# A transformer block on eight cores: x and modulation by quarters, attention with a row maximum and DMA transposes between the projection groups

## The chip, the cores and the metric

The kernel runs on the 8 cores of one Trainium2 chip. The cores share no work and no data: each takes 1024 of the 8192 tokens with a halo of 128 on either side (core r has sample r // 4, tokens from 1024 (r mod 4)). The metric is the device time of the slowest core in microseconds, the median over runs.

## The reference, cut to what matters

```python
# layer_norm, modulate, adaln as usual; adaln gives shift/scale/gate for mixer and MLP
h_ctx = modulate(ctx, mod_c[:, 0], mod_c[:, 1])
k_ctx, v_ctx = context_kv(h_ctx, w_in[l])
h = modulate(x, mod[:, 0], mod[:, 1])
mix = latent_mixer(h, k_ctx, v_ctx, rope, *mixer_params)
x = layer_norm(ALPHA * x + mod[:, 2] * mix, ln1_g[l], ln1_b[l])
ff = squared_relu_mlp(modulate(x, mod[:, 3], mod[:, 4]), w_ff1[l], w_ff2[l])
x = layer_norm(ALPHA * x + mod[:, 5] * ff, ln2_g[l], ln2_b[l])

def latent_mixer(...):
    q, k, v, u, g = split_projection(h @ w_in)      # 1024, 256, 256, 1024, 1024 columns
    q = axial_rope(q, rope); k = axial_rope(k, rope)
    attn = windowed_attention(q, k, v, k_ctx, v_ctx, sink)
    gm = chunk_spatial_gate(u, g, gln_g, gln_b, w_s, b_s)
    return jnp.concatenate([attn, gm], axis=-1) @ w_out
# windowed_attention: 8 query heads on 2 key heads; a block of 128 queries sees 384 keys
# (|i-j| <= 128 kept) and 256 context keys; one softmax over those and a sink logit.
# chunk_spatial_gate: gelu(u) * (w_s @ layer_norm(gelu(g)) + b_s), 128 positions, 8 heads
```

D_MODEL is 2048, the MLP is 8192 wide, and there is one layer.

## The kernel before

Every engine's work is written out in one order by the host program; buffers record who wrote and read them last, and each operation waits on semaphores for those (on all engines but TensorE also for earlier operations of the same engine). So the order of the source is the order of every engine and of every DMA queue. Weights are f32 in HBM and come as bf16 blocks of 2048 KB, [128, 16, 512], all on the POOL queue through `wload` (L357), into one of four slots W0 to W3 (of three, W0 to W2, from the tenth load on): the one whose last use in the plan is the oldest and that is not in use. A matmul group is 16 matmuls of 128x512 into one PSUM bank (`mm_group`, L320 on; all groups have line L324), and `bank` hands out the eight banks in turn.

- **Modulation.** `ada_chunk` (L427) multiplies one of 24 weight chunks with the two conditioning vectors; VectorE copies the sums (L443) and `ada_stage2` (L404, matmuls L410) turns them into columns. Chunks 4c to 4c+3 make vector c. Chunks 0 to 7 (shift, scale) come first. For a quarter q of the columns chunks q and 4+q are made, then ScalarE modulates four blocks of ctx (HCT) and four of x (HT; `issue_xt`, L451, loads xT on SP's queue into three buffers).
- **K, V, Q.** With chunk 2 of w_in the context's K and V, then ten token blocks of K and V; `rope` (L475) on VectorE, TensorE transposes back to head-major. Then chunks 0 and 1 for Q, 8 blocks each, modulation chunks 8 to 13 between.
- **Attention.** 16 iterations of (token block, key head), four heads at once. `at_s1` (L551) multiplies keys by queries, so that keys lie on the partitions; ScalarE takes exp with no maximum subtracted; VectorE multiplies masks in (L574). `at_s2` (L578), two iterations later, multiplies by V and by a matrix of ones for the denominators; VectorE takes a reciprocal of 128x512 (L594) and multiplies (L596). Modulation chunks 14 to 19 lie between.
- **gMLP.** u: 16 groups and Gelu into GUT. g: per token block two groups, Gelu, statistics, square root on ScalarE, normalized on VectorE (L644, L646), four plus four mixing matmuls (L657), added and multiplied on VectorE (L660, L662). The first four groups of the output projection come at the end of it.
- **Output projection.** `wout_group` (L673) for 4 column blocks x 8 token blocks, evacuated by gate, residual and statistics. The gate as a row on all partitions is made by `gate_bcast` (L716): 16 diagonals on VectorE (L722), 16 f32 matmuls with ones (L725), four copies (L727). x_tm is read by four DMAs, one for each block of 512 columns.
- **MLP.** Four passes; the first holds modulation chunks 22 and 23, both in the slot that the next weight needs, and a second `gate_bcast` before its second half. From the second half of pass 0 on nothing is touched by the change.

## Time and profile before

| | |
|---|---|
| time, median of 3 runs | 1681.81 us (1679.34 to 1687.38) |
| profiled execution: its own time, span | 1682.52 us, 1680.9 us |
| spans of the 8 cores | 1648.1 to 1680.9 us |
| PE busy | 1395.9 us (83%), 6772 matmuls |
| DVE busy | 661.5 us (39%), 1018 instructions |
| ACT busy | 266.8 us (16%), 444 |
| moved by the DMA engines | 178.66 MB, 55% of 16 engines' span |

The profile takes one execution on the slowest core. PE is TensorE, DVE VectorE, ACT ScalarE, POOL GpSimd and SP SyncE; the last two only issue DMAs here. Matmuls are pipelined, so a busy PE need not be at its peak. "clock" or PEclk is the part of full speed that TensorE was granted. A view by windows gives for stretches of the span how long each engine was busy; the timeline lists instructions in order of time, with the idle time before one and what ended it. The GB/s count bytes as written; a weight block has twice as many in HBM.

### The profile page before, as it was taken

What the parts mean: (1) busy time and instruction counts of PE and PEld (TensorE: products, weight loads), DVE (VectorE), ACT (ScalarE), POOL (GpSimd) and SP (SyncE); (2) the same over time, 40 slices, a digit from 0 to 9 for tenths busy, and PEclk for the clock granted to TensorE, in tenths of its full rate; (3) what the DMA queues carried; (4) which work ended last, traced back from release to release, by engine and by line L of the source; (5) the groups of instructions that cost most, each with busy time, mean ns of one, the idle gap of its engine ahead of it and who ended that gap; (6) DMA issues with size and microseconds to landing.
All of it is one profiled execution on the core that took longest, in us unless ns stands there. A gap on an engine that the chain in (4) does not pass through costs nothing.

```text
span 1680.9 us, 17767 instructions; the slowest of 8 cores (1648.1 to 1680.9 us)
## 1 busy us (share of the span) xinstructions
PE 1395.9 (83%) x6772; PEld 650.2 (39%) x6772; DVE 661.5 (39%) x1018; ACT 266.8 (16%) x444; POOL 37.3 (2%) x74
## 2 busy tenths in 40 slices
PE   0221387777899979979889999999999999999994
PEld 0110243332344444444344444444444444444441
DVE  0000043347722866686123431134321244222698
ACT  0111310044313400273110001100011000111000
POOL 0000000000000000000000000000000000000000
PEclk9955598779799979989989999999999999999997
DMA  9899717889823696324752253535354444445422
GB/s 157 184 184 193 214 20 131 150 135 166 144 57 62 117 246 166 64 51 70 137 95 50 51 100 57 94 61 90 64 88 69 81 75 76 82 70 109 104 89 100
DMA packets 24594, 178.66 MB, mean 106 GB/s; under 512 B 2752, under 2 KB 7616, under 8 KB 14528
## 3 DMA queue, kind: packets, MB, share of 16 engines
q0 software_dynamic: 10080, 140.94, 48.6%
q1 hardware_dynamic: 14432, 36.59, 6.4%
q8 instruction: 55, 0.90, 0.2%
q14 instruction: 27, 0.22, 0.0%
HBM read 310.07 MB, written 8.39 MB: 189 GB/s over the span
## 4 chain that ended last, share of the span: by engine, by line
PE 71%; DMA 11%; DVE 8%; another core or an unknown queue 4%; issue 3%; ACT 1%; SPq 1%; DVEq 0%; ACTq 0%; POOLq 0%
PE ps L324 68%; DMA regC<-xT 6%; DVE regD L594 2%; DMA regW<-w_in 2%; DMA regW<-w_ff 1%; DVE regA L744 1%; PE ps L725 1%; DMA regW<-w_out 1%; DMA regW<-w_ada 1%; DVE regA L838 1%; SPq L303 1%; DVE regD L833 1%; PE ps L438 1%; DVE regD L668 1%
## 5 line engine op out<-in xcount | busy, mean ns | idle before, releaser
L324 PE MATMUL ps<-regC,regW 128*128 128x512 bf16 (+1 forms) x2144 | 467.8, 381 | 27.7 <-ACT regC L313 22.0
L324 PEld LDWEIGHTS ps<-regC,regW 128*128 128x128 bf16 x2144 | 211.8, 99 | 280.5 <-issue 32.6
L324 PE MATMUL ps<-regW,regB 128*128 128x512 bf16 x960 | 228.3, 381 | 0.0
L324 PE MATMUL ps<-regW 128*128 128x512 bf16 x960 | 226.8, 379 | 0.0
L324 PE MATMUL ps<-regW,regA 128*128 128x512 bf16 x752 | 177.1, 392 | 28.4 <-DMA regW<-w_in 20.3
L313 ACT ACTIVATE regD<-ps 128x512 f32<-128x512 f32 x128 | 76.5, 597 | 713.0 <-PE ps L324 713.0
L833 DVE TENSOR_TENSOR regD<-ps,regD 128x512 f32<-128x512 f32 x128 | 88.2, 689 | 204.8 <-PE ps L324 204.8
L324 PEld LDWEIGHTS ps<-regW,regB 128*128 128x128 bf16 x960 | 94.3, 98 | 114.1 <-issue 1.7
L324 PEld LDWEIGHTS ps<-regW 128*128 128x128 bf16 x960 | 94.0, 98 | 113.4 <-issue 0.3
L324 PE MATMUL ps<-regW,regC 128*128 128x512 bf16 (+1 forms) x544 | 119.8, 382 | 3.5 <-DMA regW<-w_out 2.0
L324 PEld LDWEIGHTS ps<-regW,regA 128*128 128x128 bf16 x752 | 74.4, 101 | 118.3 <-issue 41.9
L822 DVE TENSOR_TENSOR regW<-regD 128x512 bf16<-128x512 f32 x64 | 44.3, 692 | 189.5 <-ACT regD L313 189.5
L438 PE MATMUL ps<-regW,regC 128*32 128x512 bf16 x128 | 13.1, 564 | 118.5 <-DVE regC L398 71.3
L822 DVE TENSOR_TENSOR regB<-regD 128x512 bf16<-128x512 f32 x48 | 33.3, 693 | 132.5 <-ACT regD L313 132.5
L324 PEld LDWEIGHTS ps<-regW,regC 128*128 128x128 bf16 x544 | 53.9, 100 | 66.1 <-issue 9.8
L838 DVE TENSOR_TENSOR regA<-regA,regD 128x512 f32<-128x512 f32 x96 | 66.4, 692 | 10.3 <-DVE regD L833 0.5
L313 ACT ACTIVATE regW<-ps 128x512 bf16<-128x512 f32 (+1 forms) x96 | 57.3, 598 | 71.1 <-PE ps L324 64.6
L416 DVE TENSOR_TENSOR regD<-ps,regD 128x8 f32<-128x8 f32 x24 | 3.9, 163 | 154.3 <-ACT regA L313 98.2
L594 DVE RECIPROCAL regD<-ps 128x512 f32<-128x512 f32 x16 | 53.7, 3357 | 14.8 <-PE ps L324 14.6
L324 PE MATMUL ps<-regA,regW 128*128 128x512 bf16 x256 | 55.4, 379 | 0.0
L410 PE MATMUL ps<-regD 128*128 128x2 f32 x192 | 33.4, 298 | 24.6 <-DVE regD L443 24.4
L438 PEld LDWEIGHTS ps<-regW,regC 128*32 128x32 bf16 x128 | 4.1, 122 | 124.5 <-issue 123.8
(84 smaller groups left out, 812.4 us busy)
## 6 DMA issues: line engine op xcount, KB each, us to landing
regW<-w_ff POOLq DMA_DIRECT2D x31, 2048.0 KB, 14.7
regW<-w_ada POOLq DMA_DIRECT2D x24, 2048.0 KB, 29.2
regW<-w_in POOLq DMA_DIRECT2D x7, 2048.0 KB, 16.1
regC<-xT SPq DMA_DIRECT2D x16, 640.0 KB, 20.8
regW<-w_out POOLq DMA_DIRECT2D x4, 2048.0 KB, 18.2
regA<-x_tm SPq DMA_DIRECT2D x4, 2048.0 KB, 38.3
y<-regA SPq DMA_DIRECT2D x7, 1024.0 KB, 3.9
regB<-ctxT SPq DMA_DIRECT2D x1, 2048.0 KB, 65.7
```

Of the source, the lines that this page charges most:

```text
L303: return e.dma_start(out=out_ap, in_=in_ap)
L313: return e.activation(out=out_ap, in_=in_ap, func=func, **kw)
L324: ins = te.matmul(ps_ap, lhsT=l, rhs=r, start=(i == 0), stop=(i == n - 1))
L410: ins = te.matmul(pb2.ap[:, 2 * i:2 * i + 2], lhsT=mt.ap[:, i * 128:(i + 1) * 128], rhs=SEL4.ap, start=True, stop=True)
L438: ins = te.matmul(pb.ap[32 * g:32 * g + 32, :], lhsT=lhs.ap[:, k, :], rhs=W.ap[:, k, :], start=(i == 0), stop=(i == 3), tile_position=(0, ...
L594: vec(lambda e: e.reciprocal(out=RDEN.ap, in_=pd.ap), [pd], [RDEN])
L668: vec(lambda e: e.bn_stats(out=st.ap[:, n * 6:(n + 1) * 6], in_=X[t][n].ap), [X[t][n]], [st])
L725: return te.matmul(pb.ap[:, i * 128:(i + 1) * 128], lhsT=ONESF.ap, rhs=dg.ap, start=True, stop=True)
L744: vec(lambda e: e.scalar_tensor_tensor(out=xs, in0=xs, scalar=mv.ap[:, 0:1], in1=G.ap[:, c0 * 512:c1 * 512], op0=ALU.subtract, op1=ALU.mul ...
L822: vec(lambda e: e.tensor_tensor(out=hk_.ap, in0=rl.ap, in1=rl.ap, op=ALU.mult), [rl], [hk_])
L833: vec(lambda e: e.tensor_tensor(out=tmp.ap, in0=pb.ap, in1=GATE2[n].ap, op=ALU.mult), [pb, GATE2[n]], [tmp])
L838: vec(lambda e: e.tensor_tensor(out=xb.ap, in0=xb.ap, in1=tmp.ap, op=ALU.add), [xb, tmp], [xb])
```

## The change

What it does, in the order of the program:

- cvec gets a semaphore of its own. All weights use slots W0 to W2; W3 holds the attention's buffers from the start. xT moves to the POOL queue (`load_x`), between the weights, with six buffers. Quarter q makes chunks 4+q and q, modulates four blocks of x, and adds four of the 16 partial products for K and V of token blocks 0 to 5 (`mm_part`). ctxT follows the last x, and the context's keys and values stand after the K/V groups. Constants go out on SP's queue at once.
- Attention is token-major: queries on the partitions. A step has two heads. Per head (`at_scores`) one 384-column and two 128-column matmuls, two that add the mask (0 or -1e30) through the identity, VectorE's row maximum over 640 columns, exp on ScalarE with the maximum as bias and the row's sum accumulated. A step later (`at_norm`) the row is scaled by 1/sum, on ScalarE (beside Q and g) or VectorE (beside u), into PN, and a transposing DMA on SP's queue writes it to PT. Once three pairs are normalized and not used (`at_pv`), five matmuls of 256 columns multiply by V. `at_step` does the three; one stands behind every group of Q chunk 1, every group of u, and the first of the two groups of each g block. Scores use banks 0 to 3 (two double banks), values bank 4, projections banks 5 to 7.
- gMLP: Gelu(u) goes straight into CAT; the bias of the layer norm is folded into b_s once (BB); the inverse root is three Newton steps of [128, 1] operations on VectorE; normalization is one ScalarE operation; the mix is evacuated by four operations of 128 columns and one of 512 per half.
- The gates are rows at once: the bias comes by DMA (`gate_bias`), and one f32 matmul of 128x512 with SELB adds the sums. No `gate_bcast`.
- Modulation chunks: 8 in Q chunk 0; 9, 10 in Q chunk 1; 11 to 14 in u; 15 to 17 in g; 18, 19 in the output projection; 20 to 23 in the first MLP pass. All 32 output groups stand behind g. x_tm is read by eight DMAs, one for each token block.

```diff
-        cload(CV, cvec)
+        cload(CV, cvec, grp="cv")
...
-        cload(CTXT, ctxT.rearrange("(k p) t -> p k t", p=128))
...
-            dma("sync", xs.ap, xT[k * 128:(k + 1) * 128, :], "xt%d" % (k % 3), "slot", writes=[xs])
+        def load_x(k):
+            xs = XTR[k % 6]
+            dma("gpsimd", xs.ap, xT[k * 128:(k + 1) * 128, :], "xt%d" % (k % 6), "slot", writes=[xs])
...
+        for q in range(4):
+            ada_chunk(4 + q)
+            ada_chunk(q)
+            ada_flush()
+            sl = slice(4 * q, 4 * q + 4)
+            vec(lambda e, sl=sl: e.tensor_scalar(out=MODCOL[1].ap[:, sl, :], in0=MODCOL[1].ap[:, sl, :], scalar1=1.0, scalar2=None, op0=ALU.add),
+                [MODCOL[1]], [MODCOL[1]])
+            for k in range(4 * q, 4 * q + 4):
+                load_x(k)
+                act(HT[k].ap, XTR[k % 6].ap, AF.Identity, [XTR[k % 6], MODCOL[0], MODCOL[1]], [HT[k]],
+                    bias=MODCOL[0].ap[:, k, 0:1], scale=MODCOL[1].ap[:, k, 0:1])
+            if q == 0:
+                Wkv = wload("win", 2)
+                cload(IDB, ident, "gpsimd", grp="i")
+            if q == 1:
+                cload(NEG, masks.rearrange("p (a b c) -> p a b c", a=3, b=2), "gpsimd", grp="n")
+                cload(WST, w_sT.rearrange("p (a b) -> p a b", a=8), "gpsimd", grp="s")
+            for t in range(NKP):
+                mm_part(PSB[t].ap, [(HT[k].ap[:, t * 128:(t + 1) * 128], Wkv.ap[:, k, :]) for k in range(4 * q, 4 * q + 4)],
+                        [Wkv] + HT[4 * q:4 * q + 4], PSB[t], q == 0, q == 3)
+        dma("gpsimd", CTXT.ap, ctxT.rearrange("(k p) t -> p k t", p=128), "ctx", "slot", writes=[CTXT])
...
+        def at_scores(i):
+            hk, t, p = at_pairs[i]
+            sm, sx = SM[i % 4], SX[i % 4]
+            h0 = 4 * hk + 2 * p
+            mv_ = 1 if t == 0 else (2 if t == NT - 1 else 0)
+            for a in range(2):
+                h = h0 + a
+                ps = PSD[a]
+                qa = QTall.ap[:, h, t * 128:(t + 1) * 128]
+                def fn(te, qa=qa, ps=ps):
+                    te.matmul(ps.ap[:, 0:384], lhsT=qa, rhs=KT[hk].ap[:, t * 128:(t + 3) * 128], start=True, stop=False)
+                    w = ps.ap[:, 0:384].rearrange("p (a b) -> p a b", a=3)
+                    te.matmul(w[:, 0, :], lhsT=IDB.ap, rhs=NEG.ap[:, mv_, 0, :], start=False, stop=False)
+                    te.matmul(w[:, 2, :], lhsT=IDB.ap, rhs=NEG.ap[:, mv_, 1, :], start=False, stop=True)
+                    te.matmul(ps.ap[:, 384:512], lhsT=qa, rhs=KCT.ap[:, hk, 0:128], start=True, stop=True)
+                    return te.matmul(ps.ap[:, 512:640], lhsT=qa, rhs=KCT.ap[:, hk, 128:256], start=True, stop=True)
+                P.add("tensor", fn, [QT[h], KT[hk], KCT, NEG, IDB], [ps])
+                vec(lambda e, a=a, ps=ps: e.tensor_reduce(out=sx.ap[:, a:a + 1], in_=ps.ap[:, 0:640], axis=AX.X, op=ALU.max), [ps], [sx])
+                vec(lambda e, a=a, h=h: e.tensor_scalar(out=sm.ap[:, a:a + 1], in0=sx.ap[:, a:a + 1], scalar1=-QSCALE, scalar2=NSINK8.ap[:, h:h + 1], op0=ALU.mult, op1=ALU.min),
+                    [sx, NSINK8], [sm])
+                act(PF[a].ap, ps.ap[:, 0:640], AF.Exp, [ps, sm], [PF[a], sx], bias=sm.ap[:, a:a + 1], scale=QSCALE, accum=sx.ap[:, 2 + a:3 + a])
+            vec(lambda e: e.tensor_tensor(out=sm.ap[:, 2:4], in0=sm.ap[:, 0:2], in1=SINK8.ap[:, h0:h0 + 2], op=ALU.add), [sm, SINK8], [sm])
+            act(sx.ap[:, 4:6], sm.ap[:, 2:4], AF.Exp, [sm], [sx])
+        def at_norm(i, on_act):
+            sm, sx, pn, pt = SM[i % 4], SX[i % 4], PN[i % 2], PT[i % 3]
+            vec(lambda e: e.tensor_tensor(out=sm.ap[:, 4:6], in0=sx.ap[:, 2:4], in1=sx.ap[:, 4:6], op=ALU.add), [sx], [sm])
+            vec(lambda e: e.reciprocal(out=sm.ap[:, 6:8], in_=sm.ap[:, 4:6]), [sm], [sm])
+            for a in range(2):
+                dst = pn.ap[:, a * 640:(a + 1) * 640]
+                if on_act:
+                    act(dst, PF[a].ap, AF.Identity, [PF[a], sm], [pn], scale=sm.ap[:, 6 + a:7 + a])
+                else:
+                    vec(lambda e, a=a, dst=dst: e.tensor_scalar(out=dst, in0=PF[a].ap, scalar1=sm.ap[:, 6 + a:7 + a], scalar2=None, op0=ALU.mult), [PF[a], sm], [pn])
+            def fnt(e):
+                return e.dma_start_transpose(pt.ap, pn.ap)
+            P.add("sync", fnt, [pn], [pt], dma_sem="pt%d" % (i % 3), dma_mode="slot")
...
+        def at_step(on_act):
+            st = at_state
+            if st["n"] < st["s"]:
+                at_norm(st["n"], on_act)
+                st["n"] += 1
+            if st["s"] < NP:
+                at_scores(st["s"])
+                st["s"] += 1
+            if st["v"] < st["n"] and (st["n"] - st["v"] >= 3 or st["s"] == NP):
+                at_pv(st["v"])
+                st["v"] += 1
...
+        for c in (3, 4):
+            W = wload("win", c)
+            for m in range(4):
+                h = (c - 3) * 4 + m
+                for tg in range(2):
+                    gi = 2 * h + tg
+                    pb = bank()
+                    mm_group(pb.ap, [(W.ap[:, k, m * 128:(m + 1) * 128], HT[k].ap[:, 128 + tg * 512:128 + (tg + 1) * 512]) for k in range(16)],
+                             [W] + HT, [pb])
+                    u_pend.append((pb, h, tg))
+                    at_step(False)
+                    if len(u_pend) == 2:
+                        u_evac()
+                        if gi - 1 in u_ada or gi in u_ada:
+                            ada_chunk(u_ada.get(gi - 1, u_ada.get(gi)))
+                    else:
+                        ada_flush()
+            wfree(W)
...
+        def newton_rstd(mv):
+            v, y, i0 = mv.ap[:, 1:2], mv.ap[:, 4:5], NWT.ap[:, 0:1]
+            vec(lambda e: e.tensor_scalar(out=v, in0=v, scalar1=EPS, scalar2=None, op0=ALU.add), [mv], [mv])
+            vec(lambda e: e.tensor_scalar(out=i0.bitcast(I32), in0=v.bitcast(I32), scalar1=1, scalar2=None, op0=ALU.logical_shift_right), [mv], [NWT])
+            vec(lambda e: e.tensor_scalar(out=y.bitcast(I32), in0=i0.bitcast(I32), scalar1=-1, scalar2=0x5f3759df, op0=ALU.mult, op1=ALU.add), [NWT], [mv])
+            for _ in range(3):
+                vec(lambda e: e.scalar_tensor_tensor(out=i0, in0=y, scalar=y, in1=v, op0=ALU.mult, op1=ALU.mult), [mv], [NWT])
+                vec(lambda e: e.tensor_scalar(out=i0, in0=i0, scalar1=-0.5, scalar2=1.5, op0=ALU.mult, op1=ALU.add), [NWT], [NWT])
+                vec(lambda e: e.tensor_tensor(out=y, in0=y, in1=i0, op=ALU.mult), [mv, NWT], [mv])
...
+        def g_gelu(t):
+            st, mv = ST[t], MV[t]
+            for half in range(2):
+                pb = g_pb.pop((t, half))
+                act(GG.ap[:, half * 512:(half + 1) * 512], pb.ap, AF.Gelu_apprx_tanh, [pb], [GG])
+            for half in range(2):
+                vec(lambda e, half=half: e.bn_stats(out=st.ap[:, half * 6:(half + 1) * 6], in_=GG.ap[:, half * 512:(half + 1) * 512]), [GG], [st])
+            vec(lambda e: e.bn_aggr(out=mv.ap[:, 0:2], in_=st.ap[:, 0:12]), [st], [mv])
+            newton_rstd(mv)
+            vec(lambda e: e.scalar_tensor_tensor(out=mv.ap[:, 5:6], in0=mv.ap[:, 0:1], scalar=-1.0, in1=mv.ap[:, 4:5], op0=ALU.mult, op1=ALU.mult), [mv], [mv])
+
+        def g_z(t):
+            mv, z = MV[t], GZ[t % 2]
+            act(z.ap, GG.ap, AF.Identity, [GG, mv], [z], bias=mv.ap[:, 5:6], scale=mv.ap[:, 4:5])
+
+        def g_mix(t):
+            z = GZ[t % 2]
+            for i in range(2):
+                pb = g_bank(t + 1, 2) if i == 0 else PSB[4]
+                def fnm(te, pb=pb, i=i):
+                    ins = None
+                    for hh in range(4):
+                        h = 4 * i + hh
+                        ins = te.matmul(pb.ap[:, hh * 128:(hh + 1) * 128], lhsT=z.ap[:, h * 128:(h + 1) * 128], rhs=WST.ap[:, h, :], start=True, stop=True)
+                    return ins
+                P.add("tensor", fnm, [z, WST], [pb])
+                for hh in range(4):
+                    h = 4 * i + hh
+                    vec(lambda e, pb=pb, hh=hh, h=h: e.scalar_tensor_tensor(out=TMPG.ap[:, hh * 128:(hh + 1) * 128], in0=pb.ap[:, hh * 128:(hh + 1) * 128], scalar=GCOL.ap[:, h:h + 1],
+                        in1=BB.ap[:, h * 128:(h + 1) * 128], op0=ALU.mult, op1=ALU.add), [pb, GCOL, BB], [TMPG])
+                def fnc(e, i=i):
+                    cc = CATall.ap[:, 8 + 4 * i:12 + 4 * i, t * 128:(t + 1) * 128]
...
+        g_ada = {0: 15, 2: 16, 4: 17}
+        use_banks([4])
+        for t in range(NT):
+            g_mm(t, 0)
+            ada_flush()
+            if t >= 1:
+                g_z(t - 1)
+            at_step(True)
+            g_mm(t, 1)
+            if t >= 1:
+                g_mix(t - 1)
+            g_gelu(t)
+            if t in g_ada:
+                ada_chunk(g_ada[t])
+        g_z(NT - 1)
+        wfree(*Wg)
+        while at_state["v"] < NP:
+            at_step(True)
+        use_banks(range(8))
+        Wo0 = wload("wout", 0)
+        g_mix(NT - 1)
+        for t in (5, 0, 1, 2, 3, 4, 6, 7):
...
-                gate_bcast(MODCOL[5], GATE2)
```

How the instructions stand, at three places. The POOL queue at the start, before (regW<-w_ada is a modulation chunk, regW<-w_in a projection weight):

```order
L303 DMA regW<-w_ada 128x8192 x4
L303 DMA regW<-w_ada 128x8192 [waits dma_w0,eng_tensor]
L303 DMA regW<-w_ada 128x8192 [waits dma_w1,eng_tensor]
L303 DMA regW<-w_ada 128x8192 [waits dma_w2,eng_tensor]
L303 DMA regW<-w_ada 128x8192 [waits dma_w3,eng_tensor]
L303 DMA regW<-w_in 128x8192 [waits dma_w0,eng_tensor]
```

and now:

```order
L310 DMA regW<-w_ada 128x8192 x2
L310 DMA regC<-xT 128x1280 x4
L310 DMA regW<-w_in 128x8192
L310 DMA regD<-ident 128x128
L310 DMA regW<-w_ada 128x8192 [waits dma_w0,eng_tensor]
L310 DMA regW<-w_ada 128x8192 [waits dma_w1,eng_tensor]
L310 DMA regC<-xT 128x1280 x2
L310 DMA regC<-xT 128x1280 [waits dma_xt0,eng_scalar]
```

x stands between the chunks, and K/V's weights come third. TensorE in the attention, before (one iteration: scores, values, ones, the sink):

```order
L324 MATMUL ps<-regB,regA 128x512 x5
L324 MATMUL ps<-regW,regA 128x512 x5
L324 MATMUL ps<-regW,regD 128x512 x5
L324 MATMUL ps<-regA,regD 128x512
```

and beside u now (16 matmuls of a u group, then the step's two heads and the values of an earlier pair):

```order
L333 MATMUL ps<-regA,regW 128x512 x16
L584 MATMUL psd<-regA,regB 128x384
L586 MATMUL psd<-regA,regD 128x128
L587 MATMUL psd<-regA,regD 128x128
L588 MATMUL psd<-regA,regB 128x128
L589 MATMUL psd<-regA,regB 128x128
L584 MATMUL psd<-regA,regB 128x384
L586 MATMUL psd<-regA,regD 128x128
L587 MATMUL psd<-regA,regD 128x128
L588 MATMUL psd<-regA,regB 128x128
L589 MATMUL psd<-regA,regB 128x128
L333 MATMUL ps<-regW,regA 128x256 x5
```

A group of the projection stands between two steps. VectorE in one block of g, before:

```order
L634 BN_STATS regD<-regW 128x6 x2
L635 BN_AGGR regD<-regD 128x2
L636 TENSOR_SCALAR regD<-regD 128x1
L643 RECIPROCAL regD<-regD 128x1
L644 SCALAR_TENSOR_TENSOR regW<-regW,regD 128x1024
L646 SCALAR_TENSOR_TENSOR regW<-regW,regD 128x1024
L660 TENSOR_TENSOR regW<-ps,regD 128x512
L662 TENSOR_TENSOR regC<-regW,regB 128x4x128
L660 TENSOR_TENSOR regW<-ps,regD 128x512
```

and now, the attention step and the mix (behind them come the statistics and the thirteen operations of the root):

```order
L600 TENSOR_TENSOR regD<-regD 128x2
L601 RECIPROCAL regD<-regD 128x2
L591 TENSOR_REDUCE regD<-psd 128x1
L592 TENSOR_SCALAR regD<-regD 128x1
L591 TENSOR_REDUCE regD<-psd 128x1
L592 TENSOR_SCALAR regD<-regD 128x1
L595 TENSOR_TENSOR regD<-regD 128x2
L628 CAST regC<-ps 128x2x128
L754 SCALAR_TENSOR_TENSOR regA<-ps,regD 128x128 x4
L758 TENSOR_TENSOR regC<-regA,regC 128x4x128
L754 SCALAR_TENSOR_TENSOR regA<-ps,regD 128x128 x4
L758 TENSOR_TENSOR regC<-regA,regC 128x4x128
```

## Rows read from the trace of the kernel before

**Rows 1.** The cores: us from the first to the last instruction, clock.
```profile
core 5: 1680.9 us, clock 0.918
```
**Rows 2.** Windows by stage: busy us of each engine, PEclk, DMA share, GB/s.
```profile
0.00:206.70 206.70, 33.65 (x257) 22.46 (x258) 8.54 (x25) 32.87 (x35) 7.74 (x18) 0.71 0.93 189
206.70:261.70 55.00, 41.04 (x221) 19.03 (x222) 18.27 (x53) 5.50 (x24) 1.58 (x3) 0.87 0.27 44
261.70:310.20 48.50, 38.13 (x208) 19.10 (x209) 18.82 (x36) 4.78 (x8) 1.58 (x3) 0.82 0.79 130
310.20:350.50 40.30, 38.01 (x208) 19.02 (x209) 18.66 (x35) 6.27 (x10) 1.58 (x3) 0.88 0.71 126
350.50:520.00 169.50, 145.97 (x666) 61.71 (x667) 82.62 (x78) 58.45 (x97) 3.82 (x8) 0.89 0.67 118
520.00:618.70 98.70, 87.22 (x458) 44.22 (x458) 65.34 (x118) 30.52 (x40) 2.51 (x5) 0.91 0.73 141
...
741.30:880.50 139.20, 127.40 (x602) 60.80 (x601) 57.71 (x64) 32.91 (x59) 3.17 (x6) 0.93 0.51 91
880.50:1680.90 800.40, 775.25 (x3586) 351.02 (x3583) 306.69 (x427) 58.98 (x104) 13.20 (x25) 0.98 0.42 79
```
**Rows 3.** Timeline of the attention: start us, us, engine, line, operation [idle before].
```profile
366.99 3.36 DVE L594 RECIPROCAL regD<-ps 128x512 f32<-128x512 f32 x1 [0.25 <-PE ps L324]
...
371.43 2.16 PE L324 MATMUL ps<-regW,regD 128*128 128x512 bf16 x5 [2.28 <-DVE regC L596]
```
**Rows 4.** Timeline of TensorE.
```profile
261.66 12.54 PE L324 MATMUL ps<-regW,regA 128*128 128x512 bf16 x48 [12.18 <-DMA regW<-w_in]
...
463.91 55.43 PE L324 MATMUL ps<-regA,regW 128*128 128x512 bf16 x256
...
603.79 2.50 PE L725 MATMUL ps<-regD 128*128 128x128 f32 x8 [4.11 <-DVE regD L722]
...
797.31 1.05 PE L410 MATMUL ps<-regD 128*128 128x2 f32 x8
...
807.59 57.53 PE L324 MATMUL ps<-regC,regW 128*128 128x512 bf16 x256 [5.75 <-DMA regW<-w_ff]
```
**Rows 5.** Timeline of ScalarE at the start.
```profile
68.69 1.28 ACT L313 ACT_TABLE_LOAD   x1 [68.69 <-DMA regB<-ctxT]
...
77.45 2.08 ACT L313 ACTIVATE regC<-regB,regD 128x256 bf16<-128x256 f32 x4 [7.23 <-DVE regD L460]
...
116.21 1.46 ACT L313 ACTIVATE regA<-regC,regD 128x1280 bf16<-128x1280 f32 x1 [9.62 <-DMA regC<-xT]
131.12 1.46 ACT L313 ACTIVATE regA<-regC,regD 128x1280 bf16<-128x1280 f32 x1 [13.46 <-DMA regC<-xT]
```
**Rows 6.** By tile, DMA to landing: first xT, then x_tm.
```profile
DMA to landing us min/median/max: 3.7/20.8/67.0
...
DMA to landing us min/median/max: 23.8/38.3/46.0
```
**Rows 7.** The page: what the DMA engines moved in each fortieth of the span.
```profile
GB/s 157 184 184 193 214 20 131 150 135 166 144 57 62 117 246 166 64 51 70 137 95 50 51 100 57 94 61 90 64 88 69 81 75 76 82 70 109 104 89 100
```
**Rows 8.** Timeline of VectorE in g: operations that wait for the one before.
```profile
529.85 0.21 DVE L635 BATCH_NORM_AGGREGATE regD<-regD 128x2 f32<-128x12 f32 x1
530.16 0.15 DVE L636 TENSOR_SCALAR regD<-regD 128x1 f32<-128x1 f32 x1
...
547.30 0.68 DVE L660 TENSOR_TENSOR regW<-ps,regD 128x512 f32<-128x512 f32 x1
548.09 0.69 DVE L662 TENSOR_TENSOR regC<-regW,regB 128x512 bf16<-128x512 f32 x1
```
**Rows 9.** Groups by line: count, busy us, mean ns of one, idle before.
```profile
L769 DVE TENSOR_SCALAR regC<-ps,regD 128x128 bf16<-128x128 bf16 x64 | 16.9, 335 | 5.0 <-PE ps L332 5.0
L574 DVE TENSOR_TENSOR regW<-regW,regD 128x512 bf16<-128x512 bf16 x32 | 13.5, 422 | 19.7 <-ACT regW L313 17.6 <-DVE regW L574 0.5
L512 DVE CAST regA<-ps 128x256 bf16<-128x256 f32 x10 | 4.2, 417 | 0.0
...
L313 ACT ACTIVATE regD<-ps 128x512 f32<-128x512 f32 x128 | 76.5, 597 | 713.0 <-PE ps L324 713.0
```
**Rows 10.** DMA issues: count, KB each, median us from issue to landing.
```profile
regB<-ctxT SPq DMA_DIRECT2D x1, 2048.0 KB, 65.7
...
y<-regA SPq DMA_DIRECT2D x2, 512.0 KB, 2.6
```

519 lines of the change are left out of this document (225 added, 294 removed).

## The prediction

> **What bounds the kernel now.** I read the cores first: the slowest, core 5 with a span of 1680.9 us, stands for all [rows 1]. Its execution took 1682.5 us, 1.6 us more than the span; the median of the runs shown is 1681.8, so the sum below, made against 1682.5, needs no correction. Then the windows by stage [rows 2]. From 880.5 us on TensorE is busy almost without a hole; the change leaves that part alone. What can be gained lies before. Up to 206.7 us the DMA engines are full (share 0.93) and TensorE works 34 us. From 350.5 to 520 (attention, then u) it is busy 146 of 169.5 us at clock 0.89, and VectorE is the cause: the reciprocal of the denominators takes 3.36 us, and TensorE idles 2.28 us before it may go on [rows 3]. Between stages TensorE waits for weights: 12.18 us before Q chunk 0 and 5.75 in the first MLP pass, and in each gate broadcast for VectorE's diagonals (4.11 us at its start) [rows 4]. The first broadcast fills the time from 602.6 to 618.7, the second that from 865.9 to 880.5.
>
> **1. Start up to the last HT: 206.7 to 172.** The first activation waits until 68.69 us, since its small operand shares a group semaphore with ctxT; later HT waits for xT, of which one block comes in 14.9 us (131.12 - 116.21) [rows 5], although a block can land in 3.7 [rows 6]. After the change cvec has its own semaphore, x comes in the order of its use in the one POOL queue, and ctxT and modulation chunk 8 come behind the last x. The DMA work of before is 206.7 us x 189 GB/s = 39.1 MB in 206.7 x 0.93 = 192 busy us [rows 2]. Wanted before the last HT are 9 weights of 2.1 MB, 16 x of 0.66 MB and some 3.2 MB of small tensors (now issued by SP at the very start): 32.6 MB, so 160 busy us, 167 us with the start, and 5 for the last HT: 172. Ends: the fifth slice's 214 GB/s gives 159, the second's 184 gives 184 [rows 7]; the first slice's 157 would give 215, but it holds weights (which count with half their source bytes) and ctxT's short runs only. I take the mean, which is the same kind of mix. **-35** (-48 to -20).
>
> **2. K, V and context: 55.0 to 33.** Nearly half of the K/V matmuls (72 of 160) are done behind the weights of quarters 0 to 2; 24 + 64 are left. A group of 16 takes 3.45 us (55.43 for 16 groups [rows 4]): 19, plus 4.5 for a low clock and transposes, 196. The context groups now stand behind: HCT can start when its place on ScalarE comes (about 189; ctxT has landed near 180), 16 x 0.52 = 8.3 us [rows 5], then 64 matmuls of half width, 7.3: Q starts at 205. The 12.18 us wait goes, because the load of chunk 0 no longer takes the slot that K/V holds. **-22.**
>
> **3. Q chunk 0: 48.5 to 34.** Eight groups of 3.45 with four transposes each, 3.67; one modulation chunk instead of two (1.05 for its second part, and as much for its first [rows 4]), a 2.3 us tail; chunk 1 is loaded early. **-15.**
>
> **4. Attention inside the projections.** 32 steps, each a pair of heads: eight go beside Q chunk 1, sixteen beside u, eight beside g. *TensorE* per step: scores and masks 2 x 896 columns, values 5 x 256: 3072 columns at 3.45 us for 8192, 1.3 us. *VectorE*: an operation that waits for the one before costs its duration + 0.10, so a tiny one 0.26 [rows 8]. Two maxima over 640 columns (0.82, scaled from 0.69 for 512) + 0.1, two tiny ones behind them, one more, the two of the norm, and the value copy (0.42 [rows 9] + 0.08): 1.84 + 0.52 + 0.26 + 0.52 + 0.50 = **3.64 us**. Beside u it also scales, two more over 640 columns, between 0.50 (0.42 for 512 bf16 columns) and 0.82: + 1.1 to 1.8. *ScalarE* is not the bound: 0.70 per 640 columns (0.60 for 512 [rows 9]), so 3 us of exponentials and scalings, and the projection's Gelu with its table loads.
> - Beside Q chunk 1: rope 2.5 (18.8 for eight [rows 2], with gaps) + 3.64 = 6.1 us, against 3.67 + 1.3 on TensorE. VectorE decides: 8 x 6.1 + 3 for two modulation chunks + 3 tail = 55, was 40.3. **+15.**
> - Beside u: 3.64 + 1.1 to 1.8 + about 0.4 in which the next norm waits for the sink's exponential: 5.15 to 5.85, say 5.5, against 3.45 + 1.3. 16 x 5.5 + 4 for four chunks + 3 for the gMLP bias = 95. Before, attention and u took 169.5 [rows 2]. **-74.** TensorE alone would give 80, the floor.
> - Beside g: step 3.64; the mix: 8 operations on 128 columns at 0.335 + 0.10 [rows 9], each waiting for the last because they write one buffer, and two of 0.79: 5.1; statistics 1.6 + 0.3 and thirteen tiny operations of the Newton root at 0.26: 5.3. Sum **14.0 us** against 8.6 on TensorE. 8 x 14, then 7 us until the last transposed pair has come back = 119. Before, 98.7 [rows 2], 13.8 of it output groups and 16 the gate. **+20.** If TensorE's holes pull its clock down (0.89 with holes of 2.28), its 8.6 us grow to as much as 15 and g costs 16 a period: + 16.
>
> **5. Output projection.** The four groups that stood in g come back (+13.8), two chunks come in (+4): **+18**. x_tm now comes as eight blocks of tokens; its 8.4 MB took up to 46 us before [rows 6]. Group (0,t) needs block t only, and eight banks let TensorE go on for 28 us, so I cost it at nothing; if blocks are late, a wait of up to 10 us shows at chunk 1.
>
> **6. First MLP pass: 139.2 to 121.5.** 32 x 3.45 = 110.4, four chunks 8, 3 for a late weight. The broadcast (14.6) and most of the 5.75 go; the gate's bias comes by DMA on the then empty SP queue. **-18.**
>
> Sum: -35 - 22 - 15 + 15 - 74 + 20 + 18 - 18 = -111: **1572 us**.
>
> **The unknown: the transposing DMA.** No row of before shows one. Each moves 128 x 1280 bf16 (0.33 MB), 32 of them, all on SP's queue, which has nothing else then. Values are used two steps later, so latency up to 11 us is free; but PN has two buffers and PT three, so more than one step's length *per transpose* stops the scaling, then the scores. Lower end: a 512 KB store, 2.6 us [rows 10]. Upper end: ctxT, 2048 runs of 1 KB in 65.7 us [rows 10], 32 ns a run; 128 rows in ten blocks are 1280 runs, 41 us beside four weight loads, 13.7 if a third of that is its own. Between stands xT: half of its 20.8 us for twice the bytes, 10.4, beside weights [rows 6]. I take 5 us, nearest to the store, because both begin in SBUF and most of xT's time was queueing between the weights' packets. It is then hidden. The Trainium skill (VectorE: DVE Perf Modes, The three transpose paths) gives 1309 ns for one 128x128 block through the DMA, more than three times TensorE's; ten in a row would be an estimated 13.1 us. It warns against this change; another of its pages (Advanced Engine Details and Errata, X-Bar Transpose) calls such DMAs as fast as regular ones. By the first the sum would be near rival B, by the second it stands. No run shown decides.
>
> **The rivals.**
> *A, the forecast (0.56):* VectorE is the clock of the mixer. Ends: start 159 to 184, u at 5.15 to 5.85 a step, g at 13 to 16, x_tm + 10; not all at once: 1535 to 1612.
> *C, transposes bind in part (0.24):* beside weights each takes some 8 us. Only the 24 steps beside Q and u (mean 5.7) suffer: 24 x 2.3 = 55, **1627** (1612 to 1673). For it: xT's 14.9 us a block beside weights [rows 5]. Against: ten weight loads leave gaps in these 150 us.
> *B, slower (0.13):* a transpose takes 13.7 us of its own. SP's queue is the clock of those steps: 24 x (13.7 - 5.7) = 192, **1764**. It turns slower than before from 5.7 + 111/24 = 10.3 us per transpose; about there it is no change (0.03). For it: ctxT's short runs. Against: the store.
> *D, better (0.04):* VectorE's operations overlap more than they do now, TensorE decides beside u and g stays under 13: about 1530.
> That the attention stays a stage of its own is excluded by the order of instructions: scores stand behind each projection group.
>
> **How the numbers follow.** The likeliest case gives the time, 1572. The range holds A and C and leaves out B and most of D: 1535 to 1680; A's own is 1535 to 1612. A measurement of this kernel can tell about 0.5% (8.4 us) from no change. Faster: A + C + D = 0.84; same 0.03; slower 0.13.
>
> **What would show it.** Right: cvec's activation below 10 us; last HT at 160 to 184; no long wait for w_in; beside u a period of 5.2 to 5.9 with VectorE over 90% busy or in its 0.1 us gaps; beside g 13 to 16; no gate broadcast; the last stage's 800 us unchanged. Wrong: scaling operations that wait for a DMA, or transposes that end more than 6 us apart while SP is never idle (C or B); TensorE waiting for HT after 190; a clock near half beside g.

## The result: 1805 us, slower, and where the time went

The changed kernel took 1805.03 us in the median (1757.16 to 1957.11), the kernel before 1683.24 beside it; the ratio is 1.0468 (95% 1.0401 to 1.0536). Some medians, here and below (e2's above all), hold runs in which one die ran at a lower clock; the ratios and the profiled executions leave those out. The profiled execution took 1757.16 us. The forecast was 1572 us, with 1680 as its upper end: wrong in sign and by 185 us against the profiled execution.

First the cores (span, granted clock), two of the eight:

```profile
core 2: 1702.2 us, clock 0.914
core 3: 1755.6 us, clock 0.904
```

Before, they lay between 1648.1 and 1680.9 [rows 1]; now the spread is 53 us. Something that falls differently on cores with the same program is in it; the experiments e12 and e13 show what it goes with. Then the windows of core 3, cut where the stages begin: K/V, Q chunk 0, Q chunk 1 with attention (and the gMLP bias), u with attention, g with attention, output projection, first half of MLP pass 0, the rest. Columns are the busy time of PE, PEld, DVE, ACT and POOL with instruction counts, then granted clock, DMA share, GB/s.

```profile
170.00:206.00 36.00, 30.18 (x173) 17.02 (x174) 15.96 (x51) 12.04 (x28) 0.00 (x0) 0.91 0.72 132
206.00:239.80 33.80, 31.58 (x182) 15.04 (x180) 18.31 (x34) 4.84 (x9) 1.58 (x3) 1.00 0.70 127
239.80:312.20 72.40, 50.41 (x306) 24.84 (x304) 39.90 (x96) 32.53 (x64) 1.58 (x3) 0.91 0.65 112
312.20:490.00 177.80, 106.06 (x587) 51.13 (x585) 69.53 (x178) 58.65 (x110) 3.17 (x6) 0.80 0.72 102
490.00:697.00 207.00, 101.55 (x528) 49.25 (x529) 84.96 (x273) 71.17 (x100) 2.64 (x5) 0.71 0.64 83
697.00:837.50 140.50, 126.79 (x691) 61.96 (x690) 91.60 (x201) 38.23 (x72) 3.17 (x6) 0.95 0.66 162
837.50:955.00 117.50, 117.03 (x576) 51.75 (x575) 54.23 (x47) 32.00 (x57) 3.70 (x7) 1.00 0.68 129
955.00:1755.00 800.00, 775.46 (x3593) 351.37 (x3591) 306.75 (x428) 59.57 (x105) 13.74 (x26) 0.99 0.41 82
```

Against [rows 2] and the forecast's own steps this is sharp. Q begins at 206 (forecast 205), Q chunk 1 at 239.8 (239), the output projection takes 140 us (140.4), the first half of the MLP pass 117.5 (121.5), the rest its old 800. The miss is in three rows: 72.4 us where the forecast had 58, 178 for u (92), 207 for g (119): 15 + 86 + 88, less 4 in the MLP, are the 185 us. (The window of g begins at 490; its first projection group begins at 491.1, which is the border in the table below.) In these stretches no engine is near full: beside g TensorE works 101.55 of 207 us, VectorE 85, and the clock is 0.71, so TensorE also works slowly. They are waits. The transposing DMAs, by their line (from issue to landing; who waited for them, us and times):

```profile
L609 SPq DMA_TRANSPOSE regW<-regW x32: 1237/1390/38660, 256.3 to 687.2; - x32
...
  PE ps L333: 66.3, 6
  ACT regW L322: 42.2, 1
  DVE regW L607: 25.0, 4
...
DMA to landing us min/median/max: 3.3/5.1/61.4
```

The median, 5.1 us, is the forecast's 5; the longest is 61.4. The chain that ended last shows the long ones between 290 and 490 us (start, length, what):

```profile
298.38 27.68 DMA regW<-regW
...
349.71 22.95 DMA regW<-regW
...
385.52 26.74 DMA regW<-regW
...
437.20 21.58 DMA regW<-regW
```

Four waits, 99 us, half of these 200 us of the chain. POOL issued weight loads at 296.1, 299.6, 349.95, 383.4, 393.3 and 437.4 us: each wait begins within 2.5 us of one. From 326 to 349 us no load is under way; the queues of that stretch, and of one of the longest waits (490.9 to 533), with packets, MB and share of 16 engines (q1 carries the transposes, q0 the weights):

```profile
q1 hardware_dynamic: 4597, 1.14, 25.1%
...
regW<-regW SPq DMA_TRANSPOSE x3, 3.3
```

```profile
q1 hardware_dynamic: 1410, 0.35, 64.8%
q0 software_dynamic: 130, 1.87, 46.6%
...
regW<-regW SPq DMA_TRANSPOSE x2, 52.1
```

Alone, a transpose lands in 3.3 us. Beside a weight, 1410 of its packets, about one transpose, took 42 us.

Put side by side, the landing times of all 32 transposes of this core and of the weight loads show a simple pattern. The 15 that met no weight load landed in 3.3 to 4.6 us. Each of the other 17 landed 0.3 to 3.3 us after the last weight load that it met, however early it was issued: the load issued at 437.43 us landed at 458.2, and the transposes issued at 437.20 and 444.48 landed at 458.8 and 461.5. So most of them waited for the rest of a load, 4 to 28 us. The two of 42.8 and 61.4 us met one load that itself took 52.0 us. On the other seven cores 113 of the 125 transposes that met a load landed after it in the same way.

The second fault shows where no DMA is waited for at all (start, duration, engine, line; in brackets the idle time before and its releaser):

```profile
334.16 0.82 DVE L591 TENSOR_REDUCE regD<-psd 128x1 f32<-128x640 f32 x1
...
335.39 0.80 ACT L322 ACTIVATE regD<-psd,regD 128x640 f32<-128x640 f32 x1 [3.14 <-DVE regD L592]
336.08 0.20 ACT L322 ACTIVATION_READ_ACCUMULATOR regD<-psd,regD 128x1 f32 x1
336.38 0.82 DVE L591 TENSOR_REDUCE regD<-psd 128x1 f32<-128x640 f32 x1 [1.08 <-ACT regD L322]
...
338.61 0.16 DVE L595 TENSOR_TENSOR regD<-regD 128x2 f32<-128x2 f32 x1 [1.08 <-ACT regD L322]
```

The maximum of a step's second head does not follow the first head's: it waits for the first head's exponential. `at_scores` writes both heads' maxima, row sums and biases into the same two small buffers SX and SM, and the host program orders by buffer. Beside u VectorE waits 1.08 us for that twice a step, and the second exponential follows the whole round.

### The profile page after: what moved, and what is told of

The parts are those of the page before. It is cut to its first block, busy times and chain, and to the rows that moved or that the text cites. A ratio compares the mean times of both kernels' runs of the same rounds, so it can differ in the third digit from the quotient of the medians.

```text
span 1755.6 us, 19105 instructions; the slowest of 8 cores (1702.2 to 1755.6 us)
## 1 busy us (share of the span) xinstructions
PE 1389.9 (79%) x6886; PEld 648.9 (37%) x6886; DVE 689.4 (39%) x1329; ACT 332.7 (19%) x561; POOL 47.0 (3%) x91
## 3 DMA queue, kind: packets, MB, share of 16 engines
q1 hardware_dynamic: 50192, 35.56, 10.3%
## 4 chain that ended last, share of the span: by engine, by line
PE 57%; DMA 16%; DVE 13%; issue 7%; ACT 4%; another core or an unknown queue 2%; DVEq 1%; ACTq 0%; POOL 0%; SPq 0%; POOLq 0%
PE ps L333 27%; PE psd L333 27%; DMA regW<-regW 7%; DMA regW<-w_ada 6%; DMA regC<-xT 2%; DVE regA L817 2%; ACT regD L322 2%; DVE regD L591 2%; DVE regA L754 1%; PE ps L432 1%; DVE regA L904 1%; DVE regD L899 1%; DVE regA L819 1%; ACT L322 1%
## 5 line engine op out<-in xcount | busy, mean ns | idle before, releaser
L333 PE MATMUL psd<-regC,regW 128*128 128x512 bf16 (+1 forms) x1088 | 236.9, 378 | 5.2 <-ACT regC L322 5.2
L333 PE MATMUL ps<-regC,regW 128*128 128x512 bf16 x1056 | 232.1, 380 | 0.0
L333 PE MATMUL ps<-regW,regA 128*128 128x512 bf16 (+1 forms) x640 | 150.1, 392 | 87.6 <-DMA regW<-regW 66.3
L333 PEld LDWEIGHTS psd<-regC,regW 128*128 128x128 bf16 x1088 | 106.7, 98 | 132.5 <-issue 8.0
L333 PEld LDWEIGHTS ps<-regC,regW 128*128 128x128 bf16 x1056 | 103.4, 98 | 125.4 <-issue 2.2
L333 PE MATMUL ps<-regW,regB 128*128 128x512 bf16 x480 | 113.4, 379 | 0.0
L333 PE MATMUL ps<-regW 128*128 128x512 bf16 x480 | 113.4, 379 | 0.0
L333 PE MATMUL psd<-regW 128*128 128x512 bf16 x480 | 113.4, 379 | 0.0
L333 PE MATMUL psd<-regW,regB 128*128 128x512 bf16 x480 | 113.4, 379 | 0.0
L591 DVE TENSOR_REDUCE regD<-psd 128x1 f32<-128x640 f32 x64 | 52.7, 823 | 130.6 <-ACT regD L322 95.4
```

The costliest lines, as they stand in the source:

```text
L333: ins = te.matmul(ps_ap, lhsT=l, rhs=r, start=(i == 0), stop=(i == n - 1))
L591: vec(lambda e, a=a, ps=ps: e.tensor_reduce(out=sx.ap[:, a:a + 1], in_=ps.ap[:, 0:640], axis=AX.X, op=ALU.max), [ps], [sx])
```

## The experiments

Fourteen kernels. The table has their stages from their traces (u begins; length of u, g and the output projection), the median and the ratio to the kernel before beside them. The first row is the forecast's arithmetic.

| | u begins | u | g | out. proj. | median us | ratio (95%) |
|---|---|---|---|---|---|---|
| forecast | 297 | 92 | 119 | 140 | 1572 | |
| after | 312 | 179 | 206 | 140 | 1805.0 | 1.0468 (1.0401-1.0536) |
| e1 no transposes | 311 | 158 | 160 | 154 | 1707.1 | 1.0150 (1.0116-1.0184) |
| e2 heads apart | 300 | 192 | 150 | 141 | 1809.7 | 1.0163 (1.0109-1.0218) |
| e3 both | 291 | 130 | 136 | 151 | 1639.4 | 0.9741 (0.9707-0.9775) |
| e4 fewer loads | 314 | 172 | 170 | 140 | 1714.5 | 1.0202 (1.0174-1.0230) |
| e10 = e1 + e4 | 311 | 159 | 159 | 154 | 1705.2 | 1.0171 (1.0142-1.0200) |
| e7 = e3 + Gelu ahead | 291 | 92 | 141 | 160 | 1610.4 | 0.9552 (0.9525-0.9580) |
| e8 = e3, exp for Gelu | 293 | 113 | 131 | 155 | 1617.0 (one) | |
| e9 = e7 + x_tm in queue | 294 | 91 | 139 | 146 | 1596.1 | 0.9503 (0.9486-0.9519) |
| e12 = e7 + transposes | 300 | 226 | 145 | 140 | 1736.5 | 1.0345 (1.0298-1.0392) |
| e13 = e12, plain copies | 298 | 120 | 149 | 141 | 1629.6 | 0.9705 (0.9690-0.9719) |
| e14 = e12 + e4 | 298 | 154 | 147 | 140 | 1657.9 | 0.9869 (0.9846-0.9891) |
| e5 old attention beside u | 279 | 146 | 79 | 167 | 1600.1 | 0.9489 (0.9432-0.9546) |
| e6 old attention apart | | 172 | 90 | 165 | 1632.0 | 0.9697 (0.9647-0.9748) |
| e11 = e5 + x_tm in queue | 280 | 144 | 79 | 155 | 1582.5 | 0.9427 (0.9410-0.9445) |

For e8 the time of the profiled execution stands in place of the median (before beside it: 1684.6). For e6 "u" is attention and u together; for e5 and e11 attention lies wholly beside u, with its last two iterations behind the sixteenth group. u ends where the first projection group of g begins. (The expectation of e14 gives 237.8 us for u of e12; that counts the first two groups of g to u.) By a limit of 2%, e1, e10 and e14 are no change against the kernel before, and e2 and e4 lie too near the limit to call.

### The two faults, apart and together (e1, e2, e3)

e1: `at_norm` writes into PT itself and the transposing DMA is left out, so that the values' matmuls read untransposed rows.

```diff
-            sm, sx, pn, pt = SM[i % 4], SX[i % 4], PN[i % 2], PT[i % 3]
+            sm, sx, pt = SM[i % 4], SX[i % 4], PT[i % 3]
+            pn = pt
...
-                return e.dma_start_transpose(pt.ap, pn.ap)
```

> Left out: the transposing DMA; ScalarE or VectorE scale straight into PT and the values multiply what lies there untransposed. Theory S (starved transposes: a transpose lands in 3.3 to 5 us alone, and only when the load ends beside a weight load, 17 to 28 us): the waits for it go, and what is left is the undisturbed period, 7.7 us beside u and 18.9 beside g: 178 - 127 and 207 - 156, so 100 us less, about 1650, and no wait over 5 us in the mixer. Theory H (the two heads of a step wait for each other through one small buffer, and this chain is the clock): hardly any change, above 1730.

e2: the same bytes, but a buffer for each head's maximum (XA), bias (MA) and sum (SA).

```diff
-                vec(lambda e, a=a, ps=ps: e.tensor_reduce(out=sx.ap[:, a:a + 1], in_=ps.ap[:, 0:640], axis=AX.X, op=ALU.max), [ps], [sx])
+                vec(lambda e, a=a, ps=ps: e.tensor_reduce(out=sx.ap[:, a:a + 1], in_=ps.ap[:, 0:640], axis=AX.X, op=ALU.max), [ps], [XA[(i % 4, a)]])
...
-                act(PF[a].ap, ps.ap[:, 0:640], AF.Exp, [ps, sm], [PF[a], sx], bias=sm.ap[:, a:a + 1], scale=QSCALE, accum=sx.ap[:, 2 + a:3 + a])
+                act(PF[a].ap, ps.ap[:, 0:640], AF.Exp, [ps, MA[(i % 4, a)]], [PF[a], SA[(i % 4, a)]], bias=sm.ap[:, a:a + 1], scale=QSCALE, accum=sx.ap[:, 2 + a:3 + a])
```

> The maxima, negated maxima and sums of the two heads of a step get buffers of their own (same bytes, no dependence between the heads). Theory H: the second maximum no longer waits 1.08 us for the first head's exponential, nor the sum behind it; 2.2 us less in each of 32 steps, about 1690. Theory S: the transposes are the clock, each shorter step waits longer for them; 0 to 20 us less, 1735 to 1757.

e3 makes both edits.

> e1 and e2 together; left out again: the transposing DMA. If both theories hold and add up: Q chunk 1, u and g at the forecast's 6.1, 5.5 and 14 to 16 us a period, 1575 to 1605. If S alone matters: as e1, within 10 us.

Each alone is worth some 3% of before, both together 7.3% (1.0468 to 0.9741). That is 1.0% more than their sum, which is about what the four intervals allow by chance, so it isn't shown that each fault partly hid the other. e2's stages shift as well: g falls from 206 to 150 us, but u grows from 179 to 192. In after the wait of 42 us lies in g; in e2 the longest, a transpose that took 64.8 us, lies in u. e3 beats the kernel before, and it still misses the forecast by 67 us: u takes 130 us, not 92.

### Weight loads and transposes hold each other up (e4, e10)

e4 leaves out the loads of modulation chunks 9 to 17 (their matmuls stay and read whatever the slot holds); e10 does that to e1.

```diff
-            W = wload("ada", n)
+            W = wload("ada", n, not 9 <= n <= 17)
```

> Left out: the loads of modulation chunks 9 to 17 (their matmuls stay and use what lies in the slot), so the mixer has 5 or 6 weight loads where it had 14; the transposes stay. Theory S: the long waits for transposes stay only beside w_in and the first w_out, 60 to 100 us less, 1660 to 1700. If a transpose is slow of itself, or H is the clock: less than 20 us less.

> After without the transposing DMAs (as e1) and without the loads of modulation chunks 9 to 17 (as e4). Alone, e1 took 3.1% and e4 2.6% off after. Theory S (weight loads cost time only by starving the transposing DMAs): with the transposes gone the loads cost nothing, so this is e1 again, 1695-1707, 1.010-1.016 of before. Rival (the loads cost time by themselves, as late weights): the two add up, 1655-1670, 0.985-0.99.

Nine loads fewer are worth 2.6% with the transposes there, and nothing without them (e10 1.0171, e1 1.0150, stages alike to 2 us). So in after the loads cost their time through the transposes, and none by coming late themselves. In e4 the transposes' median landing time is 3.4 us, the longest 27.3.

### What was left of u: ScalarE's order (e7, e8)

e3's timeline beside u:

```profile
370.03 0.79 ACT L331 ACTIVATE regD<-psd,regD 128x640 f32<-128x640 f32 x1 [3.12 <-DVE regD L601]
...
372.08 1.28 ACT L331 ACT_TABLE_LOAD   x1
...
373.37 1.08 ACT L331 ACTIVATE regC<-ps 128x512 bf16<-128x512 f32 x2
...
374.11 1.24 PE L342 MATMUL ps<-regA,regW 128*128 128x512 bf16 x5 [0.91 <-ACT regC L331]
```

The Gelus of two finished projection groups stand on ScalarE behind the step's two exponentials, which wait for VectorE's maxima, which wait for scores that TensorE takes up only after the groups; and the next groups wait for the bank that the Gelu frees. That is a ring through three engines, and TensorE stood up to 5.5 us in it. e7 puts the Gelus ahead of the step; e8 takes the exponential for Gelu, so that no table is changed.

```diff
-                    at_step(False)
-                    if len(u_pend) == 2:
+                    full = len(u_pend) == 2
+                    if full:
                         u_evac()
+                    at_step(False)
```

```diff
-                act(CATall.ap[:, 8 + h, tg * 512:(tg + 1) * 512], pb.ap, AF.Gelu_apprx_tanh, [pb], CAT[8 + h][4 * tg:4 * tg + 4])
+                act(CATall.ap[:, 8 + h, tg * 512:(tg + 1) * 512], pb.ap, AF.Exp, [pb], CAT[8 + h][4 * tg:4 * tg + 4])
```

> As e3 (no transposing DMA, small buffers a head), and beside u the two Gelu activations of a pair of projection groups are put ahead of the attention step on ScalarE, not behind it. In e3 a step beside u took 8.1 us where the forecast had 5.5, and TensorE stood 5.1 to 5.7 us before every second pair of groups, released by the Gelu. Theory R (a ring through ScalarE's order: groups, scores, maximum, exponential, table load, Gelu, bank free, groups): the Gelu now runs while VectorE takes the maxima, so the ring opens, the u stretch falls from 130 to 100-112 us (6.3 to 7 a step) and the time is 1609-1620, 0.956-0.964 of before. Rival V (VectorE's own work decides, its dependent operations cost more than counted): 8.1 a step stays, 1635-1642, 0.972 or more.

> As e3, with the exponential in place of Gelu for u and g (other values, the same shapes), so that ScalarE never changes its table in the mixer. Theory R with table loads as a part of the ring: beside u two loads of 1.28 us fall on the ring of two steps (16.2 us), 8 x 2.56 = 20 us less there, and beside g two loads a period, 8 x 2.56 = 20 us less: 1599-1610, 0.951-0.957. If the loads are hidden in ScalarE's waits (rival): less than 8 us, 1631-1640, 0.97 or more.

PE's waits for the Gelu's buffer beside u, e3 and then e7 (us, times, longest), and e7's window of u:

```profile
PE ps L342 <- ACT regC L331: 16.6, 4, 5.5
PE ps L441 <- ACT regC L331: 10.2, 2, 5.1
```

```profile
PE ps L342 <- ACT regC L331: 0.5, 2, 0.3
...
291.00:383.00 92.00, 87.19 (x577) 47.45 (x586) 65.31 (x169) 55.10 (x106) 3.21 (x6) 0.97 0.84 135
```

u takes 92 us, the forecast's 95 less the 3 for the gMLP bias, at 5.75 us a step; TensorE is busy 87 of them. Theory R held, with more gained than it gave (it had 100 to 112 us); V fell. But the forecast had VectorE at over 90% there, and it works 65 of 92 us: the 5.5 us a step came out right by luck, with the wrong engine as the clock. e8 has u at 113 us: the two table loads are 17 of the 38 us that the ring cost, and about 4 us beside g, where 8 periods were expected to give 20.

### What the transposes cost a kernel without other faults (e12, e13, e14)

e12 is e7 with the transposing DMAs back. e13 is e12 with a plain copy in their place, e14 is e12 without the nine loads.

```diff
-                return e.dma_start_transpose(pt.ap, pn.ap)
+                return e.dma_start(out=pt.ap, in_=pn.ap.rearrange("p (a b) -> p a b", a=10))
```

> As e7 (buffers apart for the two heads, Gelu ahead of the step), but with the transposing DMAs of after: what they cost once the mixer's ring is open. Theory S (starved beside weights): the weight loads beside u stand closer now, each holds a transpose 17 to 40 us while two to four steps of 5.8 us go by, so 7 to 9 waits of 5 to 25 us: 60 to 90 us over e7, 1670-1700, about before itself. Rival (the latency is hidden as two steps ahead, what e1 gained was something else): 1610-1630.

> As e12, with a plain copy between the same two buffers (128 partitions, ten blocks of 256 bytes, same bytes, same queue, same waits) in place of each transposing DMA; the values are then not transposed. Theory T (what makes these DMAs slow beside the weights is their form: pieces of a transpose that each engine must work through one by one, 1312 packets each and the engines busy at 17 to 55 GB/s): a plain copy is as harmless as other small transfers, u takes 92-115 us and the time is 1605-1640, 0.955-0.975 of before. Theory Q (any transfer on SP's queue that must be back within two steps is starved beside 2 MB weight loads): u stays above 180 us, 1690 or more, above 1.0 of before.

> As e12 (with its transposing DMAs), without the loads of modulation chunks 9 to 17. Theory S (a transpose and a weight load hold each other up): the projection weights of u and g remain, one beside u, two beside g's start, so two or three of e12's long waits remain; u 237.8 falls to 115-150, time 1625-1660, 0.967-0.988 of before. Rival (the transposes alone are too slow for a step of 5.8 us, loads or not): above 1700, 1.012 or more.

The transposes cost the mended kernel 126 us (1736.5 against 1610.4), more than twice their 3% in after and more than I expected. Line and waiters in e12:

```profile
L618 SPq DMA_TRANSPOSE regW<-regW x32: 1237/1748/61878, 251.7 to 661.5; - x32
...
  PE ps L342: 154.9, 6
  DVE regW L616: 134.3, 5
...
DMA to landing us min/median/max: 3.3/5.1/70.6
```

The copies move the same bytes, on the same queue, with the same waits, and cost 19 us. Both sums hide some of the loss, because with a slower mixer the wait for x_tm goes (the output projection takes 140 us in both, 160 in e7): in u and g together the transposes cost 138 us, the copies 36. Packets and MB of the hardware queue in the whole run of e7, e13 and e12:

```profile
q1 hardware_dynamic: 8208, 25.07, 4.7%
```

```profile
q1 hardware_dynamic: 12816, 35.55, 6.3%
```

```profile
q1 hardware_dynamic: 50192, 35.56, 12.9%
```

A copy is (12816 - 8208) / 32 = 144 packets, a transpose (50192 - 8208) / 32 = 1312, for the same 0.33 MB. So theory T held for the time (1629.6, in its range), and u at 120 us just misses its 92 to 115. The copies aren't free: on the profiled core 12 of the 22 that met a weight load landed only after it, and the longest took 22.3 us. What only the transposes show is the load that becomes long itself. In e13 and in e7 no weight load of the mixer took over 31 us on any core. In e12 one of 50 to 62 us stands on cores 0, 3, 4 and 7 (spans 1693 to 1730 us) and none over 32 on cores 1, 2, 5 and 6 (spans 1648 to 1658). So the spread of the cores, and with it the time of the slowest, goes with that long load. Cores 2 and 3 of e12, with the landing times of their modulation chunks in the mixer:

```profile
core 2: 1652.0 us, clock 0.925
...
DMA to landing us min/median/max: 12.4/16.2/24.2
```

```profile
core 3: 1713.4 us, clock 0.905
...
DMA to landing us min/median/max: 12.4/17.6/56.2
```

A transpose and a copy differ in two things, the transposing and the number of packets; which of them does the harm is open. (e1, e3, e7 to e10 and e13 transpose nothing, e4, e10 and e14 leave loads out, and e8 has other values: they are measurements, not kernels to use.) With the nine loads gone (e14) 79 of the 126 us come back; the loads of w_in remain, one of them took 60.1 us on the profiled core, and u, at 154 us, is just above the 115 to 150 expected.

### x_tm, and the parts outside the mixer (e9, e5, e6, e11)

e9, e7 with one more edit, moves the eight x_tm loads into POOL's queue and the chunks 18 and 19 later. e5 and e6 keep the change's start, gates and weight order, with the attention and g of the kernel before; in e5 one iteration stands beside each u group, in e6 all stand ahead of u. e11 is e5 with e9's edit.

```diff
-            dma("sync", Xall.ap[:, t, :], x_tm[t * 128:(t + 1) * 128, :], "x%d" % t, "slot", writes=X[t])
+            dma("gpsimd", Xall.ap[:, t, :], x_tm[t * 128:(t + 1) * 128, :], "x%d" % t, "slot", writes=X[t])
...
-        wo_ada = {(0, 3): 18, (1, 3): 19}
+        wo_ada = {(1, 1): 18, (2, 1): 19}
```

And e6 against e5 (in e5, `at_s1` and, two groups later, `at_s2` stand behind each u group):

```diff
-        at_q = []
+        pipeline(2 * NT, at_s1, at_s2, depth=2)
...
-                    at_q.append((gi, at_s1(gi)))
-                    if len(at_q) > 2:
-                        at_s2(*at_q.pop(0))
```

> As e7, with the eight x_tm blocks in POOL's queue, ahead of modulation chunk 18 and of output weight 1, and chunks 18 and 19 eleven projection groups... six groups later. In e7 the output projection took 160 us, in after 140: there VectorE waited 23.9 us for x_tm blocks that came beside two weight loads, and TensorE stood 13.25 us behind it. If that wait is the 20 us: output projection 140-148, time 1590-1600, 0.945-0.951 of before. If x_tm is bound by the DMA engines' total (8.4 MB and the weights in the same 60 us) the wait moves to output weight 1: 1605-1612, no gain over e7.

> The start, the gates and the weight order of after, but the attention of before (keys on partitions, no maximum, no transposes; reciprocal 3.36 us on VectorE) and its g stage; one attention iteration goes beside each of the sixteen u groups. If steps 1, 2, 3, 5 and 6 of the prediction are right on their own, all that is left to differ is attention with u: before 169.5 us of which TensorE worked 146. So 239 + 40 + 150 (146 to 160) + 69 to 75 for g + 140 + 118 + 801.6 = 1557 to 1575, about 1562, 0.928 of before. Rival (interleaving itself costs, whatever the attention: banks, order of the queues): no better than e6.

> As e5, with the attention of before as a stage of its own ahead of u. Attention and u then take the 169.5 us of before: 1570-1600, about 1583, 0.941 of before, 15 to 24 us above e5. This is what the change's parts outside the mixer are worth alone: the forecast had -35 -22 -15 (start, K/V, Q chunk 0), the gate's 16 us in g and -18 in the MLP pass, together -106 against before, less 2 where tails differ. If it comes out above 1620, those parts were not right either and only looked so.

> As e5 (1600), with x_tm in POOL's queue as in e9. In e5 the output projection took 167 us, in after 140. If its x_tm wait goes: 1572-1585, 0.935-0.942 of before, the fastest kernel of the study. If it only moves: 1595-1602.

Once the mixer is quicker, x_tm comes together with a modulation weight and an output weight. This row of VectorE's waits is e7's; e9 has none like it:

```profile
DVE regA L783 <- DMA regA<-x_tm: 23.9, 5, 8.1
```

The output projection falls from 160 to 146 us, and the time from 1610 to 1596. The forecast had "a wait of up to 10 us" there, and it is 20; in after it didn't show: there both weights were issued (662 and 667 us) 24.7 us or more before x_tm (691.7), and both had landed by then.

e5 came out 38 us above what I expected and e6 49. In both, 25 us or more of that lie in the output projection, which waits for x_tm; g is above its 69 to 75 us by some 4 in e5 and 15 in e6, of which 9.1 us are a late w_in block. That taking the four output groups out of g saved less than the 13.8 us that I had counted may be part of it; no run shows that. By the expectation of e6, a time above 1620 means that the parts outside the mixer were not all right, and 1632 says so: the start, K/V, Q chunk 0 and the MLP pass were, the output projection and part of g were not. Still both beat the kernel before: the parts outside the mixer are worth 3.0% alone (e6), where the forecast's terms for them had some 6%, and laying the old attention beside u another 2.1% (attention and u 146 us, not 172). **e11, at 1582.5 us and 0.9427, is the fastest kernel of the study, and beats both**: the old key-major attention, which needs no transposes, in the new frame. Three of its windows (attention with u, g, output projection):

```profile
280.00:424.40 144.40, 125.77 (x607) 52.36 (x604) 73.77 (x70) 76.31 (x112) 3.18 (x6) 0.99 0.65 113
424.40:503.00 78.60, 66.18 (x394) 33.03 (x394) 61.55 (x92) 30.43 (x39) 5.77 (x12) 0.96 0.71 144
503.00:658.00 155.00, 133.20 (x689) 62.56 (x688) 92.57 (x199) 36.42 (x70) 4.25 (x9) 0.90 0.77 154
```

## Why the prediction was wrong, step by step

**1. Start: right.** The activation of cvec no longer waits for ctxT, and the last HT ends at 168.46 + 1.45 = 169.9 us (forecast 172):

```profile
4.18 1.28 ACT L322 ACT_TABLE_LOAD   x1 [4.18 <-DMA regD<-cvec]
...
168.46 1.45 ACT L322 ACTIVATE regA<-regC,regD 128x1280 bf16<-128x1280 f32 x1 [0.25 <-DMA regC<-xT]
```

**2 and 3. K/V, context, Q chunk 0: right**, 36 and 33.8 us for 33 and 34, and the wait for w_in ahead of Q chunk 0 is gone.

**4. Attention inside the projections: wrong, and all of the miss.** It gave 55 + 95 + 119 = 269 us and got 457. Two of the signs that it named for being wrong showed: scaling operations that wait for a DMA (25.0 us in four waits), and a low clock beside g (0.71). Four things failed in it, in order of size.
- *"I take 5 us, nearest to the store"* for a transpose, as one value for all 32. The median was 5.1 us, and that says nothing: the 3.3 us alone and the wait for a weight load to land, up to 61 us, are two different things, and the steps wait for the long ones. The step that failed is "It is then hidden". Both outer bounds stood in the text (2.6 and 41 us, the latter from ctxT's 1 KB runs beside weights [rows 10]), and fourteen weight loads fall into the mixer: the term should have been the number of loads that meet a transpose, each stopping the steps until it has landed. Worth 3.2% in after, 7.9% in the mended kernel.
- *"Two maxima ... + 0.1, two tiny ones behind them"*: I added VectorE's operations up one behind the other and did not look at which buffers they name. The shared SX and SM put ScalarE's exponential between the maxima. It was in the source, and in front of me: the prediction used the same rule for the mix ("because they write one buffer"). Worth 3.1%, and 4.3 us in each of g's periods: without a modulation chunk z, the normalized g, begins every 18.4 us in after and in e1, every 14.1 in e2 and e3. After and then e3:

```profile
664.11 1.24 ACT L322 ACTIVATE regA<-regA,regD 128x1024 bf16<-128x1024 f32 x1 [7.85 <-DVE regD L600]
682.53 1.24 ACT L322 ACTIVATE regA<-regA,regD 128x1024 bf16<-128x1024 f32 x1 [7.84 <-DVE regD L600]
```

```profile
537.29 1.24 ACT L331 ACTIVATE regA<-regA,regD 128x1024 bf16<-128x1024 f32 x1 [5.59 <-DVE regD L611]
551.42 1.24 ACT L331 ACTIVATE regA<-regA,regD 128x1024 bf16<-128x1024 f32 x1 [5.59 <-DVE regD L611]
```

- *"ScalarE is not the bound"*: its busy time isn't (57 of 130 us in e3), but its place in a ring is. 38 us of u (e7).
- *"14.0 us ... 8 x 14, then 7"* beside g: the period is right, 14.13 us in e3. Left out were the three modulation chunks that stand in g (17.36 us from z to z with two of them, so 3.2 more each, and 19.04 with the first) and the first z, 19.6 us after g's start. That makes g 136 to 141 us even in the mended kernels, not 119; this is most of the 24 us by which e9 (1596) still misses 1572.

**5 and 6. Output projection and MLP pass: right** in after (140.5 and 117.5), the first in part because the mixer was slow; the x_tm wait was underrated.

**The rivals.** B, given 0.13, lies near the profiled execution with its 1764 us by luck. It had the transposes slow one by one, at 13.7 us of their own; they are 3.3 us of their own, and far more where a weight load meets them. Nor do they turn the sign alone: without them (e1) the kernel is still at 1.0150; only in the mended kernel do they (0.9552 to 1.0345). C had the place (beside weights), and priced it at 8 us. Neither had the shared buffers, without which after would have been at 1.016. The Trainium skill's 1309 ns for a block (VectorE: DVE Perf Modes, The three transpose paths), ten in a row 13.1 us by my estimate, is not what the trace shows: ten blocks land in 3.3 us when nothing else moves. The Trainium skill also has such transfers as fast as regular ones (Advanced Engine Details and Errata, X-Bar Transpose): alone the transpose took 3.3 us and the copy 2.4, the shortest of e12 and of e13, so the transpose is slower by 0.9 us; beside weight loads the two are far apart, e12 and e13 differ by 107 us.

## What to carry to other kernels

Price a DMA on the path by what else its engines carry at that moment: here a transpose of 3.3 us beside a 2 MB load landed only when the load had, so a median of landing times is no price. Before adding up an engine's operations, write down the buffers each names, and walk the ring through all engines once: two waits of 1 us, or two activations in the wrong order, cost more here than the operations themselves. When one stage gets quicker, ask which loads now fall together.

## What the runs showed of the hardware

- A transposing DMA of 128x1280 bf16 within SBUF makes 1312 packets of 256 bytes, where a copy makes 144. Undisturbed, the record of a packet lasts 23 x 16 x 0.251 / 4597 = 0.020 us (326 to 349 us of after). In the wait from 490.9 to 533 us it was 42.1 x 16 x 0.648 / 1410 = 0.31 us. The two queues' shares add up to 1.11 there, so records overlap and hold waiting as well as work, while the DMA engines moved 53 GB/s. The harm is mutual: the queue of the weights moved 1.87 MB in these 42 us, and the load issued at 480.70 us took 52.0 us. The longest modulation chunk in the mixer took 26.2 us in e7 and 25.5 in e13, without transposes, and 60.5 on the profiled core of e12.
- The Trainium skill (DMA: Bandwidth & Descriptors, Queues, rings and completion order) says that an engine takes turns between its queues, a packet at a time, and that a packet holds some 9 to 17 descriptors. The profile counts 1410 short to 130 long pieces in one stretch, 11 to 1; whether these are such packets or descriptors no run shows, so the counts speak neither for nor against turns, and the mechanism of the slowing stays open. Whether a transpose made by TensorE would have been cheaper wasn't tried.
- The victims vary: with the same program and no shared data, e12's cores spanned 1648 to 1730 us, by whether a long load stood on them, e11's 1570 to 1583.
